# The end of a hybrid decoder layer: the last RMSNorm of the MLP and its residual, scheduled another way

## The reference

```python
def rmsnorm(x, g):
    xf = x.astype(jnp.float32)
    y = xf * lax.rsqrt(jnp.mean(xf * xf, axis=-1, keepdims=True) + EPS)
    return (y * g.astype(jnp.float32)).astype(x.dtype)
...
    h2 = rmsnorm(x, g_pre_mlp)
    f = jnp.square(jax.nn.relu(h2 @ w_ff1)) @ w_ff2
    x = x + rmsnorm(f, g_post_mlp)
```

## Time and profile before

| what | value |
|---|---|
| median of 3 runs | 2119.84 us (2118.01 to 2120.25) |
| the profiled execution, its own time | 2114.53 us |
| its span in the profile | 2112.4 us |
| PE busy | 1989.2 us, 94% of the span |
| DVE, ACT, POOL busy | 933.0, 619.6, 908.2 us |
| mean granted clock of TensorE | 0.968 of full speed |

### The profile page before, as it was taken

The page is one execution under the profiler, slowest core; times in us unless marked ns, Lnnn a source line. Parts: engine busy times, 40 slices in busy tenths (PEclk is TensorE's granted clock), DMA queues, the critical chain, the costliest instruction groups (busy, mean ns, idle before and its releaser), DMA issues.

```text
span 2112.4 us, 33914 instructions
## 1 busy us (share of the span) xinstructions
PE 1989.2 (94%) x13137; PEld 1943.9 (92%) x13137; DVE 933.0 (44%) x1977; ACT 619.6 (29%) x1172; POOL 908.2 (43%) x528
## 2 busy tenths in 40 slices
PE   5799999999999999999989989879999989999995
PEld 3699999999999999999979979879999989999994
DVE  6601553045502552045577772776667640011127
ACT  4411220122111220122126535654444443222120
POOL 4453233422333223332332226567777744444313
PEclk8799999999999999999979999999999999999998
DMA  3121332123311331123544325322232343222402
GB/s 141 60 91 41 122 127 76 40 87 128 111 41 41 140 128 57 51 81 134 204 155 151 106 90 190 111 81 103 99 121 87 105 163 119 99 82 100 161 31 80
DMA packets 89289, 218.27 MB, mean 103 GB/s; under 512 B 7720, under 2 KB 40744, under 8 KB 88792
## 3 DMA queue, kind: packets, MB, share of 16 engines
q1 hardware_dynamic: 78784, 192.48, 26.5%
q10 hardware_dynamic: 10392, 24.14, 3.2%
HBM read 162.93 MB, written 53.66 MB: 103 GB/s over the span
## 4 chain that ended last, share of the span: by engine, by line
PE 85%; DVE 7%; issue 3%; ACT 3%; POOL 1%; DMA 1%; DVEq 0%; SPq 0%; ACTq 0%; POOLq 0%
PE bank L839 76%; PE bank L967 1%; PE bank L970 1%; DVE x_in L1634 1%; PE bank L1155 1%; DVE acc L1634 1%; PE bank L959 1%; PE bank L922 1%; PE bank L965 1%; DMA x_in<-xT 1%; PE bank L1137 0%; PE bank L1039 0%; PE bank L946 0%; PE bank L1062 0%; PE bank L1006 0%
## 5 line engine op out<-in xcount | busy, mean ns | idle before, releaser
L839 PE MATMUL bank<-h_hi,w_hi 128*128 128x344 f32 (+1 forms) x2072 | 663.7, 320 | 30.5 <-DVE h_lo L1649 13.7
L839 PE MATMUL bank<-h_lo,w_hi 128*128 128x344 f32 (+1 forms) x2072 | 648.8, 313 | 0.0
L839 PE MATMUL bank<-h_hi,w_lo 128*128 128x344 f32 (+1 forms) x2072 | 647.2, 312 | 0.0
L675 POOL TENSOR_TENSOR w_hi<-w_raw,ones 128x1024 fp32r<-128x1024 f32 x84 | 159.2, 1896 | 702.9 <-PE bank L839 690.0
L839 PEld LDWEIGHTS bank<-h_hi,w_hi 128*128 128x128 f32 x2072 | 395.6, 191 | 36.9 <-DVE h_lo L1649 14.3
L839 PEld LDWEIGHTS bank<-h_hi,w_lo 128*128 128x128 f32 x2072 | 395.5, 191 | 1.0
L839 PEld LDWEIGHTS bank<-h_lo,w_hi 128*128 128x128 f32 x2072 | 395.2, 191 | 0.0
L677 POOL TENSOR_TENSOR w_lo<-w_raw,w_hi 128x1024 fp32r<-128x1024 f32 x84 | 202.8, 2414 | 6.6
L2106 DVE TENSOR_TENSOR acc<-acc,bank 128x344 f32<-128x344 f32 x72 | 36.9, 512 | 300.5 <-PE bank L839 300.5
L1185 ACT ACTIVATE side_t<-bank 128x344 f32<-128x344 f32 x96 | 44.0, 458 | 284.0 <-PE bank L839 284.0
L839 PE MATMUL bank<-f_hi,w_hi 128*128 128x344 f32 x384 | 123.2, 321 | 0.7 <-DVE acc L2106 0.7
(11 more groups left out here) (418 smaller groups left out, 4438.5 us busy)
## 6 DMA issues: line engine op xcount, KB each, us to landing
w_raw<-w_stream SPq DMA_DIRECT2D x113, 512.0 KB, 3.7
d_side<-side_t ACTq DMA_DIRECT2D x32, 516.0 KB, 2.7
f_raw<-d_f SPq DMA_DIRECT2D x24, 516.0 KB, 4.8
gates<-d_side SPq DMA_DIRECT2D x24, 344.0 KB, 4.4
d_f<-sq SPq DMA_DIRECT2D x16, 516.0 KB, 3.9
dC<-stC SPq DMA_DIRECT2D x32, 256.0 KB, 3.7
qkb<-d_qk SPq DMA_DIRECT2D x32, 256.0 KB, 4.0
o_C_s<-dC SPq DMA_DIRECT2D x32, 256.0 KB, 2.0
```

The source lines that it names most:

```text
L675: pool.tensor_tensor(w_hi[:, slot, :], w_raw[:, slot, :], ones[:, 0:1].to_broadcast([P, 1024]), ALU.mult).then_inc(s_hi_made, 1)
L839: last = pe.matmul(out, st, mv, start=i == 0, stop=i == n - 1)
```

## The change

1. `f_mean(0)` and `f_mean(1)` move one block forward on TensorE, from behind blocks 17 and 21 to behind blocks 16 and 20. The roots on ACT move from i = 18 and 22 to i = 16 and 20, the reciprocals on DVE too, the scales to i = 17 and 18 (21 and 22), and both groups' adds to the end of i = 18 and 22.
2. DVE no longer adds the squares of blocks 15, 19 and 23 to `frb`. `f_mean(g)` is now two accumulating float32 matmuls: ones by `frb`, and ones by the slot of `fsq` that holds the last square. `f_sums` counts the sums that are left. `square_f(18)` and `square_f(22)` wait for the mean, since TensorE now reads their slot.
3. The reciprocal is written to the PSUM bank of the mean, and the scales read it there; `frs` is gone.
4. In group 2 POOL adds rows 0 to 3 and DVE rows 4 to 7, in place of 5 and 3. The stores are cut in the same way.

```diff
@@ f_sums, y_pool
+        def f_sums(i):
+            return i + 1 - sum(q <= i for q in (15, 19, 23))
+        y_pool = (5, 5, 4)
...
@@ SP
             for g in range(NG):
-                sp.wait_ge(s_y_ready_pool, 5 * (g + 1))
-                sp.dma_start(o_y[:, 0:5, tok[g]], x1_back[:, 0:5, tok[g]]).then_inc(s_y_stored, 16)
-                sp.wait_ge(s_y_ready, (KD - 5) * (g + 1))
-                sp.dma_start(o_y[:, 5:KD, tok[g]], x1_back[:, 5:KD, tok[g]]).then_inc(s_y_stored, 16)
+                m = y_pool[g]
+                sp.wait_ge(s_y_ready_pool, sum(y_pool[:g + 1]))
+                sp.dma_start(o_y[:, 0:m, tok[g]], x1_back[:, 0:m, tok[g]]).then_inc(s_y_stored, 16)
+                sp.wait_ge(s_y_ready, KD * (g + 1) - sum(y_pool[:g + 1]))
+                sp.dma_start(o_y[:, m:KD, tok[g]], x1_back[:, m:KD, tok[g]]).then_inc(s_y_stored, 16)
...
@@ POOL
-                for k in range(5):
+                for k in range(y_pool[g]):
...
@@ TensorE
             def f_mean(g):
-                pe.wait_ge(s_f_summed, 16 + 4 * g)
-                pe.matmul((b_I, b_U, b_S)[g][:, 0:G], ones[:, :], frb[:, tok[g]], start=True, stop=True).then_inc(s_f_ssq, 1)
+                i = 15 + 4 * g
+                pe.wait_ge(s_f_summed, f_sums(i))
+                pe.matmul((b_I, b_U, b_S)[g][:, 0:G], ones[:, :], frb[:, tok[g]], start=True, stop=False)
+                pe.wait_ge(s_f_squared, i + 1)
+                pe.matmul((b_I, b_U, b_S)[g][:, 0:G], ones[:, :], fsq[:, i % 3, :], start=False, stop=True).then_inc(s_f_ssq, 1)
...
-                    if g and u == 29:
+                    if g and u == 28:
                         f_mean(g - 1)
...
@@ ACT
-                if i >= 3:
-                    act.wait_ge(s_f_summed, i - 2)
+                if i in (18, 22):
+                    act.wait_ge(s_f_ssq, (i - 14) // 4)
+                elif i >= 3:
+                    act.wait_ge(s_f_summed, f_sums(i - 3))
...
-                if i in (18, 22):
-                    f_root((i - 18) // 4)
+                if i in (16, 20):
+                    f_root((i - 16) // 4)
...
@@ DVE
-                step(dve.reciprocal(frs[:, tok[g]], frb[:, tok[g]]))
+                step(dve.reciprocal((b_I, b_U, b_S)[g][:, 0:G], frb[:, tok[g]]))
...
-                    stt(acc[:, k, tok[g]], acc[:, k, tok[g]], vcol(V_FF + k), frs[:, tok[g]], ALU.mult, ALU.mult)\
+                    stt(acc[:, k, tok[g]], acc[:, k, tok[g]], vcol(V_FF + k), (b_I, b_U, b_S)[g][:, 0:G], ALU.mult, ALU.mult)\
...
-                for k in range(5, KD):
+                for k in range(y_pool[g], KD):
...
                 ff2_add(24 + j, g, j >= 4 and j % 2 == 1)
-                if i:
+                if i not in (0, 16, 20):
                     add_square(i - 1)
-                if i in (18, 22):
-                    q = (i - 18) // 4
+                q = i // 4 - 4
+                if i in (16, 20):
                     y_inverse(q)
+                elif i in (17, 21):
                     y_scale(q, range(4))
-                elif i in (19, 23):
-                    q = (i - 19) // 4
+                elif i in (18, 22):
                     y_scale(q, range(4, KD))
-                    if q == 0:
-                        y_add(0)
-            add_square(23)
-            y_add(1)
+                    y_add(q)
             y_inverse(2)
             y_scale(2, range(KD))
             y_add(2)
```

More of the change, by code:

```diff
@@ L126, in hybrid_layer @@
          (f1_hi, f1_lo),
-         (_q1, fsq, frb, frs),
+         (_q1, fsq, frb),
          (_q2, bC_hraw, bC_raw, _q4, _q5, wcA_raw),
@@ L149, in hybrid_layer @@
             [("f1_hi", [P, KD, N], F32R), ("f1_lo", [P, KD, N], F32R)],
-            [("_q1", [P, 16 * N], F32), ("fsq", [P, NG, G], F32), ("frb", [P, N], F32), ("frs", [P, N], F32)],
+            [("_q1", [P, 16 * N], F32), ("fsq", [P, NG, G], F32), ("frb", [P, N], F32)],
             [("_q2", [P, 12 * N], F32), ("bC_hraw", [P, 4, HALF], F32), ("bC_raw", [P, 4, HALF], F32), ("_q4", [P, NG, G], F32),
@@ L2120, in add_square @@
                     prev = max(q for q in range(i) if f_last[q][1] == g)
-                    dve.wait_ge(s_f_summed, prev + 1)
+                    dve.wait_ge(s_f_summed, f_sums(prev))
                     dve.tensor_tensor(frb[:, tok[g]], frb[:, tok[g]], fsq[:, i % 3, :], ALU.add).then_inc(s_f_summed, 1)
```

## The result

The changed kernel takes 2110.32 us in the median (8 runs, 2103.38 to 2116.19), the kernel before 2120.05 (8 runs, 2114.77 to 2124.89). The ratio is 0.995, with a 95% interval of 0.9933 to 0.9967: 0.5% faster, some 9.7 us.

What follows compares the result with a forecast made beforehand. TensorE was taken to carry 85% of the span, with DVE binding the end. A first scale 6.65 us earlier plus 2.3 us in the tail make 8.95 us: median 2119.84 to 2110.9, range 2107.8 to 2115.2.

Steps and rivals of the forecast that it cites:

- DVE is the bound of the end: After block 17 DVE is late; in group 2 eight scales take 7.25 us because POOL works beside them.
- rival A: Scales in groups 1 and 2: POOL and DVE collide as before despite the bank; gain only 5.0 us, 2114.8; chance 10%.
- The price of a PSUM operand: Scales reading the reciprocal from PSUM: 0.49 us from start to start; the skill's fixed cycles would take 0.8 us off.
- A mean in front of a block: TensorE before blocks 17 and 21: a two-matmul mean costs 1.44 us, 0.86 for the first and 0.58 for the second.
- Slack of root and reciprocal: Groups 0 and 1: the reciprocal ends 1.2 us before DVE's next add is allowed, so root and reciprocal are covered.
- DVE behind A18: DVE from the add of block 18: add, sum, four scales and three adds make 4.1 us against the block's 3.77.
- TensorE's last sum: End of group 2: a second matmul replaces DVE's 0.43 us sum; both inputs ready within 0.1 us, mean 1.43 us.
- no wait of TensorE over 1 us: Sign of a right forecast: from block 16 on, TensorE never waits longer than 1 us.
- Tail: From group 2's first scale to the span's end: 2.3 us gained, between 2.1 (first store decides) and 2.6 (last issue).
- C: Groups 0 and 1: moved means wait for squares, or reciprocal and root hold blocks 18 and 22; 2118 to 2120; chance 4%.
- B: End less steep: last mean at the 1.2 GHz level (+1.26) or POOL's adds stay at 1.15 (+0.9); 2112.8; chance 13%.
- D: TensorE's clock drops in group 2 to the 1.2 GHz level, +6 us for its four blocks; 2126; chance 3%.

Runs made afterwards that it cites:

- a fourth execution: Kernel before, with all eight residual adds of group 2 on DVE after the scales and none on POOL: stage 69.13 us against 67.98.

## Why the prediction was right, step by step

Predicted 2110.9 (2107.8 to 2115.2), measured 2110.32; predicted gain 8.95, measured 9.49 in the stage. That the medians meet within 0.6 us is partly luck, since single runs of the changed kernel lie between 2103 and 2116 us; the stage and its parts are the better test.

- **DVE is the bound of the end, and its scales are what makes it so.** Right, and shown both ways: PSUM alone gives 5.93 us; taking POOL away gives 3.99 us for scales in SBUF. Undone in the changed kernel the PSUM operand costs 3.64 (rival A had put that case at 4.0), so its worth overlaps with that of the order: 5.93 + 3.74 + 0.07 = 9.74 for those parts on their own is over the 9.49 of all four.
- **The price of a PSUM operand.** I took 0.49 from start to start; 3.96 us for eight are that. The Trainium skill (VectorE: DVE Perf Modes, "The TRN2 errata — SBUF-src ops pay a fixed extra latency per instruction") gives a PSUM source 62 fixed cycles more at 0.96 GHz, by estimate 65 ns for each scale. That isn't seen: 3.96 us with the PSUM operand, 3.99 with the SBUF one. The reciprocal takes 2.31 us into the bank, 2.30 before.
- **A mean in front of a block.** Mis-sized. I took 1.44 us, 0.86 of it for the first matmul from 4.63 − 3.77. Measured 4.99 − 3.77 = 1.22, 0.58 for each matmul. The 4.63 had a mean in it and an even unit's wait; after, without a mean, block 18 comes 4.64 us behind block 17. So 0.86 was the price of the wait, and the mean was wholly hidden in it. This is 0.4 us of the 0.54 by which I was low, and the reading that TensorE ends 0.4 us later fell with it: from the add of block 13 its last block ended 42.9 us on before and 42.8 after.
- **Slack of root and reciprocal.** The sum through block 14 is done during block 16, behind block 15's add, and not during block 15 as I wrote; at 2058.8 it is still over 2 us ahead of the mean at 2061.6. The slack was right: the reciprocal ends at 2065.7 and the add of 17 comes at 2066.63, DVE idle for 0.94 (predicted 1.2).
- **DVE behind A18.** Predicted 4.1 for blocks 19 and 23, measured 4.07 and 4.07.
- **TensorE's last sum.** Its timing was right, but not where it pays: at the end it is worth 0.07 us, since the matmul costs what the sum did. It is worth 1.4 in groups 0 and 1. The sign "no wait of TensorE over 1 us" was wrong, against my own sum of 1.3 us ahead of the last mean; that wait was 1.33.
- **From the add of 23 to the first scale.** 5.34 by my steps, 5.38 measured, clock 1.00.
- **Tail.** 9.95 predicted, 10.00 measured. Of my two cases (first issue or last issue sets the end) the runs decide for the first; POOL's adds take 0.87 from start to start, I had 0.9 (the line through my two rows gives 0.95). "With 5 and 3 POOL would end last" was wrong, by my own numbers too: in that run POOL's store goes at +5.33 and DVE's at +6.13, and what counts is that POOL's goes 1.1 us later.
- **Rivals.** A and C didn't come. The half clock of B did not come in the changed kernel. It came in the last mean of the kernels with the PSUM operand alone and the order alone, behind waits of 5.93 and 3.35 us, and not in the changed kernel with the SBUF reciprocal, behind 2.75 us. D didn't come; but the evidence that I set against it, a wait of 2.6 us that left the clock at 1.00, was one trace; two more agree with it, but a fourth execution with the same wait lost 1.46 us. What speaks for the changed kernel is another number: its longest wait of TensorE in the stage is 1.33 us, and in both its traces the clock was 1.00 behind it.

## What to carry to other kernels

When VectorE and GpSimd work side by side, give VectorE's instructions at most one SBUF tensor: an operand that all of a group share (here the reciprocal) can live in PSUM; here that cost nothing and made eight scales 3.3 us cheaper. When two stores end a kernel and the second is issued before the first is through (here up to 2.1 us behind it, with a first store of 688 or 860 KB), the first one's issue sets the end; look for a gap between the transfers. Compare a stage by its own length in the timeline when its start wanders by more than the effect.

## What the runs showed of the hardware that was not expected

- The same wait of 2.6 us of TensorE left the granted clock at 1.00 in three executions (twice the kernel before, once with the split alone: 4.79 us from block 21 to 22) and brought it to 0.50 in a fourth, for 1.46 us. Why isn't settled.
- The stage of the two kernels profiled twice repeats to 0.02 us, but it began between 2044.4 and 2051.0 us in thirteen traces of kernels that are the same ahead of it. Before and after are alike up to some 850 us (a long row of matmuls starts at 854.06 and 853.92) and 5 us apart by 1260 (1256.33 and 1261.48). What shifts there isn't settled. Between the two traces of the kernel before it is all of the difference (4.9 us of span, the same stage).
